# Halves of the split weight blocks over the contraction instead of the columns, in a kernel of two model blocks on one core

## What is computed

```python
for l in range(2):
    mod = silu(c) @ w_ada[l] + b_ada[l]
    shift, scale, gate = split(mod)
    h = rms_norm(x, g_pre[l]) * (1 + scale) + shift
    (cq, ckv, kr, za, qb, kb, vb, zb, qc, kc, vc, zc, gcols) = split_cols(h @ w_in[l], IN_SPLITS)
    o_a = (mla_branch(cq, ckv, kr, ...) * silu(za)) @ w_o_mla[l]
    o_b = (swa_branch(qb, kb, vb, ...) * silu(zb)) @ w_o_swa[l]
    o_c = (diff_branch(qc, kc, vc, ...) * silu(zc)) @ w_o_diff[l]
    g = sigmoid(gcols).reshape(B, S, 3, D)
    y = (g[:, :, 0] * o_a + g[:, :, 1] * o_b + g[:, :, 2] * o_c) @ w_out[l]
    x = x + gate * rms_norm(y, g_post[l])
```

## Time and profile before

| | us |
|---|---|
| median of 3 runs | 1274.35 |
| lowest and highest run | 1274.13, 1277.66 |
| the profiled execution | 1275.58 |
| its span, first to last instruction | 1273.7 |
| busy in the span: PE | 1176.4 |
| PEld | 907.3 |
| DVE | 666.0 |
| ACT | 430.2 |
| POOL | 285.7 |

### The profile page before, as it was taken

The page is one execution under the profiler, slowest core; times in us unless marked ns, Lnnn a source line. Parts: engine busy times, 40 slices in busy tenths (PEclk is TensorE's granted clock), DMA queues, the critical chain, the costliest instruction groups (busy, mean ns, idle before and its releaser), DMA issues.

```text
span 1273.7 us, 18043 instructions
## 1 busy us (share of the span) xinstructions
PE 1176.4 (92%) x7403; PEld 907.3 (71%) x7403; DVE 666.0 (52%) x1091; ACT 430.2 (34%) x1041; POOL 285.7 (22%) x275
## 2 busy tenths in 40 slices
PE   7999999999897799789979999999898999999987
PEld 6888754677675422132268999998788799899877
DVE  3755866333883200010072556577785255667875
ACT  4759542334643200000055413304324431320432
POOL 0322331330510200000032122242452113224240
PEclk9999999999899899999989999999998999999999
DMA  7433435786129999999984444253321535334310
GB/s 214 175 133 125 160 99 165 270 292 237 68 83 416 410 422 421 421 421 421 413 193 140 155 158 166 99 199 133 132 98 65 188 110 195 141 116 157 125 67 33
DMA packets 94692, 255.97 MB, mean 201 GB/s; under 512 B 9873, under 2 KB 16322, under 8 KB 82322
## 3 DMA queue, kind: packets, MB, share of 16 engines
q1 hardware_dynamic: 90844, 251.18, 53.5%
q0 software_dynamic: 1152, 3.06, 0.8%
q10 hardware_dynamic: 2614, 0.59, 0.3%
HBM read 251.96 MB, written 2.59 MB: 200 GB/s over the span
## 4 chain that ended last, share of the span: by engine, by line
PE 61%; DVE 16%; DMA 12%; ACT 6%; SPq 2%; issue 2%; POOL 1%; ACTq 0%; DVEq 0%; POOLq 0%
PE bank L771 57%; DVE ring_r L2171 3%; PE bank L780 3%; DVE acc L2276 3%; SPq L691 2%; DMA place<-in_w_gate_dram 2%; DMA w_hi<-in_w_gate_dram 2%; DMA ring<-in_w_down_dram 2%; DMA ring<-in_w_up_dram 2%; DMA ring<-in_w_out_dram 1%; ACT L1644 1%; DMA ring<-in_w_ada_dram 1%; DVE ring L2286 1%; ACT ring L1644 1%; ACT oa L1644 1%
## 5 line engine op out<-in xcount | busy, mean ns | idle before, releaser
L2987 POOL CAST w_hi_r<-ring 128x1024 fp32r<-128x1024 f32 x136 | 151.9, 1145 | 629.0 <-DMA ring<-in_w_in_dram 258.3
L771 PE MATMUL bank<-ring_r,xT_hi 128*128 128x256 f32 (+1 forms) x864 | 242.6, 281 | 0.0
L2171 DVE TENSOR_TENSOR ring_r<-ring,w_hi_r 128x1024 fp32r<-128x1024 f32 x136 | 184.9, 1389 | 52.0 <-POOL w_hi_r L2987 52.0
L771 PE MATMUL bank<-w_hi_r,xT_hi 128*128 128x256 f32 x704 | 204.7, 291 | 6.8 <-DVE xT_r L2176 3.7
L771 PE MATMUL bank<-w_hi_r,xT_r 128*128 128x256 f32 x704 | 199.4, 283 | 0.0
L771 PEld LDWEIGHTS bank<-ring_r,xT_hi 128*128 128x128 f32 x864 | 164.7, 191 | 0.2
L771 PEld LDWEIGHTS bank<-w_hi_r,xT_hi 128*128 128x128 f32 x704 | 133.7, 190 | 19.0 <-issue 9.3
L771 PEld LDWEIGHTS bank<-w_hi_r,xT_r 128*128 128x128 f32 x704 | 133.2, 189 | 0.0
L771 PE MATMUL bank<-xT,ring 128*128 128x256 f32 x576 | 126.4, 380 | 0.0
L771 PEld LDWEIGHTS bank<-xT,ring 128*128 128x128 f32 x576 | 109.2, 191 | 15.3 <-issue 0.6
L2276 DVE SCALAR_TENSOR_TENSOR acc<-raw,cols,acc 128x256 f32<-128x256 f32 x168 | 87.9, 530 | 28.9 <-ACT acc L1644 23.8
(11 more groups left out here) (403 smaller groups left out, 2237.7 us busy)
## 6 DMA issues: line engine op xcount, KB each, us to landing
ring<-in_w_in_dram SPq DMA_DIRECT2D x38, 2048.0 KB, 7.8
ring<-in_w_ada_dram SPq DMA_DIRECT2D x12, 2048.0 KB, 8.8
ring<-in_w_up_dram SPq DMA_DIRECT2D x22, 1024.0 KB, 26.1
ring<-in_w_down_dram SPq DMA_DIRECT2D x20, 1024.0 KB, 25.3
ring<-in_w_gate_dram SPq DMA_DIRECT2D x18, 1024.0 KB, 20.9
ring<-in_w_out_dram SPq DMA_DIRECT2D x8, 2048.0 KB, 7.8
place<-in_w_gate_dram SPq DMA_DIRECT2D x6, 1024.0 KB, 26.8
bias<-in_w_up_dram SPq DMA_DIRECT2D x6, 1024.0 KB, 26.2
```

Source lines behind the costliest of these rows:

```text
L771: return release(nc.tensor.matmul(o, lhsT, rhs, start=start, stop=stop))
L2171: tt(lo, raw_, hi.bitcast(F32), ALU.subtract).then_inc(lo_done.sem, lo_done.one("piece"))
L2987: nc.gpsimd.tensor_copy(hi, raw_).then_inc(hi_done.sem, hi_done.one("piece"))
```

## The change

`by_rows(block)` is new. It holds for blocks of more than 2,048 elements a partition that are `w_out_2`, or `w_in_2` without the three blocks of `channel_job`. For them a part is no longer half of the columns over 8 k, but 4 k (`KH`) over all columns: part 0 is k 0 to 3, part 1 is k 4 to 7, each with one run of 2,048 elements in the ring. `row_sums` computes the 4 k of part `c` for a token tile into the whole width of the bank, starting the sum at k = 0 and ending it at k = 7, so a bank's sum now runs over both parts. `gate_sums`, `first_jobs`, the sections that aren't transposed, and `w_out_2` use it. A group is then 4 k by 3 matmuls, 12 in a row, of 512 columns (416 in the block at column 512). In `first_jobs` the wait for a tile's second half of k (x1 or x3) stands before k = 4, which is now the first matmul of part 1; in the very first part the wait for its second piece stands before k = 2. Pieces follow the parts: 2 k of 512 columns. Loads, homes, slots and the numbers of parts and pieces stay as they are.

```diff
--- before.py
+++ after.py
@@ -185,6 +185,13 @@
 
 
 SPLIT = ("w_in_2", "w_o_mla_2", "w_o_swa_2", "w_o_diff_2", "w_out_2")
+KH = DK // 2
+
+
+def by_rows(block):
+
+    name, _, _, k, c0, w = block
+    return k * w > HI and (name == "w_out_2" or name == "w_in_2" and c0 not in (SECTIONS[1][0][0], SECTIONS[2][0][0], SECTIONS[2][1][0]))
 
 
 SECTIONS = [[(0, 512), (512, 416)], [(928, 512), (1440, 256), (1696, 512)],
@@ -459,6 +466,9 @@
 
             n, i, m = parts_of[h]
             nk, w = plan[n][3], plan[n][5]
+            if by_rows(plan[n]):
+                return [v[slot[n]][:, i * KH * w:(i + 1) * KH * w].rearrange("p (k n) -> p k n", k=KH)
+                        for v in (ring, ring_r)] + [homes[hi_home[h][0]][:, 0:KH * w].rearrange("p (k n) -> p k n", k=KH)]
             return [v[slot[n]][:, 0:nk * w].rearrange("p (k n) -> p k n", k=nk)[:, :, i * w // m:(i + 1) * w // m]
                     for v in (ring, ring_r)] + [homes[hi_home[h][0]][:, 0:nk * w // m].rearrange("p (k n) -> p k n", k=nk)]
 
@@ -1345,11 +1355,16 @@
                                    k == 0, k == DK - 1)
                 last.then_inc(pj_pe.sem, pj_pe.one("job"))
 
+            def row_sums(w, t, c, o):
+
+                for k in range(KH * c, KH * c + KH):
+                    last = mm3(o, at(xs, every, k, slice(t * P, (t + 1) * P)), at(w, every, k - KH * c),
+                               k == 0, k == DK - 1)
+                return last
+
             def gate_sums(w, t, c, o):
 
-                for k in range(DK):
-                    last = mm3(o[:, c * T:(c + 1) * T], at(xs, every, k, slice(t * P, (t + 1) * P)), at(w, every, k),
-                               k == 0, k == DK - 1)
+                last = row_sums(w, t, c, o[:])
                 if c:
                     last.then_inc(gt_pe.sem, gt_pe.one("group"))
 
@@ -1388,12 +1403,12 @@
                     for c in range(m):
                         if t == 0:
                             ws.append(next_part(1 if part[0] == 0 else 2))
-                        for k in range(DK):
-                            if ws is sections[0] and c == 0 and k == DK // 2:
+                        for k in range(KH * c, KH * c + KH):
+                            if ws is sections[0] and k == KH:
                                 pe.wait_ge(xs_dve.sem, xs_dve.at(f"x{2 * t + 1}", l))
-                                if l == t == 0:
-                                    pe.wait_ge(lo_done.sem, 2)
-                            last = mm3(o[:, c * n // m:(c + 1) * n // m], at(xs, every, k, slice(t * P, (t + 1) * P)), at(ws[c], every, k),
+                            if ws is sections[0] and l == t == 0 and k == KH // 2:
+                                pe.wait_ge(lo_done.sem, 2)
+                            last = mm3(o[:, 0:n], at(xs, every, k, slice(t * P, (t + 1) * P)), at(ws[c], every, k - KH * c),
                                        k == 0, k == DK - 1)
                         if t:
                             part_read()
@@ -1436,11 +1451,8 @@
                             o = [job_bank(), job_bank(1)]
                             for c in range(m):
                                 w = next_part()
-                                n = section[0][2] // m
                                 for t in range(TT):
-                                    for k in range(DK):
-                                        last = mm3(o[t][:, c * n:(c + 1) * n], at(xs, every, k, slice(t * P, (t + 1) * P)),
-                                                   at(w, every, k), k == 0, k == DK - 1)
+                                    last = row_sums(w, t, c, o[t][:, 0:section[0][2]])
                                     if c == m - 1:
                                         last.then_inc(pj_pe.sem, pj_pe.one("job"))
                                 part_read()
@@ -1622,9 +1634,7 @@
                                 ws.append(next_part())
                             elif l < L2 - 1 and half and c:
                                 normed_transposes(l + 1, 0)
-                            for k in range(DK):
-                                last = mm3(bank[4 + 2 * half + t][:, c * T:(c + 1) * T], at(xs, every, k, slice(t * P, (t + 1) * P)),
-                                           at(ws[2 * half + c], every, k), k == 0, k == DK - 1)
+                            last = row_sums(ws[2 * half + c], t, c, bank[4 + 2 * half + t][:])
                             if t:
                                 part_read()
                         last.then_inc(w2_pe.sem, w2_pe.one("q"))
```

## The result

The changed kernel took 1267.47 us (median of 4 runs, 1266.24 to 1268.76), the kernel before 1275.05 beside it (4 runs, 1274.13 to 1277.66): ratio 0.9933, 95% interval 0.9914 to 0.9952 (the plain quotient of the two medians is 0.9941; ratios in this text are the record's). By the medians that is 7.6 us less. 1270.0 had been predicted, 4.4 us less. The gain is 1.7 times the forecast one by the medians and 1.9 times by the ratio, so terms of the sum were too small. Which ones is the subject of what follows. The profiled execution took 1266.58 us, its span 1264.8.

What follows compares the result with a forecast made beforehand. TensorE was taken to bound the attention units and last projection, DVE's weight split the stretch between the layers. Four terms summed to 4.4 us (1.3 to 5.4), from 1274.35 to 1270.0 us, range 1266.6 to 1273.8.

Steps and rivals of the forecast that it cites:

- The price of a pair: Two 256-column matmuls cost 0.2354 to 0.2370 us, one of 512 costs 0.2344: 0.0018 us saved a pair (0.0010 to 0.0026).
- Term 1: 38 groups in unbroken TensorE rows on the chain (first section, early gates, section blocks, w_out_2): 0.8 us saved (0.5 to 1.2).
- Term 2: 40 groups between the short matmuls of attention units, 0.04 us saved each: 1.6 us (0.8 to 2.0).
- Term 3: 416-column block for the second token tile, two groups a layer, 0.38 us saved each: 1.5 us (0 to 1.5).
- Term 4: 416-column block's second half, first token tile, layer 1, at the lower clock after idle: 0.5 us saved (0 to 0.7).
- What was put at nothing: Rest of the first tile's openings, other w_out_2 and gate groups, moved waits, DVE's and POOL's single runs, later releases: no effect.
- the signs that the prediction had named against itself: Wide steps above 0.237 us reading the ring, over 6 TensorE waits for the split, or the hole growing beyond TensorE's earlier saving.
- it only waits longer: Between the layers the chain runs over DVE's weight split, so a shorter TensorE group there saves nothing.
- Columns alone count: Rival: 416 columns cost twice 208, and a unit's group saves only 0.02 us; 1.6 us saved, 1272.7 us; chance 0.20.
- A clock episode vanishes: Rival: one low-clock episode after an idle, worth 1.4 us, disappears; 5.9 us saved, 1268.5 us; chance 0.10.
- A wide matmul steps like a narrow one: Rival: 512 columns step by 0.118 us, so 78 groups save 110 us, giving 1164 us; chance 0.01.
- The collision of DVE and POOL: Rival: single-run splits make both engines collide, 0.84 us more for each of 17 pieces on the chain; 1284.2 us; chance 0.06.

Runs made afterwards that it cites:

- e8: The changed kernel with unused rows of 48 matmuls of each width, 128 to 512 columns, added behind its last matmul: 1361.69 us (one run).
- e1: The changed kernel with its row halves kept, but wide products issued as two narrow ones again, except bank openers: 1275.18 us, ratio 1.0003 to the kernel before.
- e2: The kernel before with only the 416-column block cut by rows and multiplied wide: 1273.62 us, ratio 0.9983 to the kernel before.
- e4: The changed kernel unaltered, run again beside the kernel before: 1267.76 us, ratio 0.9939.
- e7: The changed kernel unaltered, run once more in the next batch, beside the filled kernels: 1266.82 us, ratio 0.9942 to the kernel before.
- e5: The changed kernel with unused matmuls filling TensorE's idle before two projections and in layer 1's opening: 1265.61 us, ratio 0.9928 to the kernel before.
- e6: The kernel before with the same idle places filled, by narrow matmuls in the opening: 1272.65 us, ratio 0.9983 to the kernel before.
- e11: The changed kernel with attention tiles moved by 32 bytes and the idle places filled: 1268.21 us, ratio 0.9933 to the kernel before.
- e12: As e11, with the expert stage's tiles moved to multiples of 64 bytes as well: 1268.69 us, ratio 0.9938 to the kernel before.

## Why the prediction was wrong in its size, and right in its direction

**The price of a pair** is the step that failed: 0.0018 us was taken (0.0010 to 0.0026), and the runs show 0.005 to 0.010. Both numbers of the difference were read from rows that don't stand for the others. "In rows 5 the 512-column form, which the branch output projection already has, goes 48 steps from 742.80 to 754.05: 0.2344" is true of that projection and was carried over to matmuls with another stationary tile, which step by 0.2300 (0.232 in the last projection). And the narrow step was taken from a unit and from the last projection, 0.1177 and 0.1185, where the long row from 757.00 steps by 0.1200. An error of 2% in one of two numbers of this size is several times their difference. "The time goes by columns, not by instructions" fell with it: e8 shows a fixed part, and e1 that the number of matmuls is the gain.

The terms can be measured in the profiled pair by how much earlier the same matmul starts.

**Term 1**, 0.8 us (0.5 to 1.2): mis-sized, and outside its bounds. The pieces that hold its 38 groups became 2.7 us shorter, without the 416-column block's share, 0.07 a group. The last projection gave 0.49 for 8 groups (23.03 to 22.54 us, where 22.7 to 22.8 had been forecast). The eight groups of the two section blocks gave 0.94 in layer 0 and 0.37 in layer 1: pieces of 37.07 and 39.84 us, then 36.73 and 39.61, all became 36.60 and 39.37. That is the narrow form's two steps: the rows within these pieces stepped by 0.1200 in layer 0 and by 0.1178 in layer 1. So part of this gain is that of one execution.

**Term 2**, 1.6 us (0.8 to 2.0): 1.7 was measured, by luck. Two errors cancel. In branches 0 and 1 a unit's piece became 0.06 shorter (its group 2.88 instead of 2.93 us), and 24 groups gave 1.5. In branch 2 sixteen groups gave 0.16 together, since TensorE does not set the pace there. DVE's last work on the probabilities of a unit there and the transposes that read them, before and after:

```profile
891.75 0.48 DVE L2733 SCALAR_TENSOR_TENSOR prob<-prob,ssum 128x256 f32<-128x256 f32 x1
...
892.29 0.44 PE L780 MATMUL bank<-eye,prob 128*128 128x128 f32 x2
```

```profile
887.72 0.48 DVE L2743 SCALAR_TENSOR_TENSOR prob<-prob,ssum 128x256 f32<-128x256 f32 x1
...
888.26 0.44 PE L790 MATMUL bank<-eye,prob 128*128 128x128 f32 x2
```

The transposes start 0.06 us behind DVE both times, and 0.21 us (before) and 0.38 us (after) behind the start of the last matmul of the gate group, where in branch 1 it is one step, 0.12 and 0.23. The unit takes 4.47 us before (887.82 to 892.29) and 4.48 after (883.78 to 888.26). The chain shows TensorE pieces all the same, because the last matmul's row still covers so short a wait: this is where the prediction's reading that a shorter group shortens the kernel in the units was wrong.

**Term 3**, 1.5 us: right. The step of 416 columns is 0.189 (0.1905 taken), a group 0.40 (0.38 taken), 1.6 us in all, and e2 agrees.

**Term 4**, 0.5 us: right in this pair, by luck in part. The block's second half took 4.31 us from 966.62 to 970.93, just as worked out, against 4.95; with a step of 0.346 at the lower level (0.345 taken). But the clock came back sooner elsewhere: 3.65 us for the same 12 in e4.

The four terms as measured are 2.7 + 1.7 + 1.6 + 0.6 = 6.6 us, beside the 6.5 of the pair. The median moved by 7.6, 7.5 (e4) and 7.4 (e7). The clock may account for some of the 0.9 that is left: one episode costs about 1.5 us and comes at one place or another in more than half of the cases. The narrow form's step may account for some too. Whether the changed kernel has fewer episodes by its own doing stays open: its executions had 0.983 to 0.985, 0.985 to 0.986 and 0.981 to 0.985 in three batches.

**What was put at nothing** stayed there, or nearly. DVE's and POOL's lines, as in the earlier trace rows, and TensorE's wait for the split, as in the earlier trace rows:

```profile
L2181 DVE TENSOR_TENSOR ring_r<-ring,w_hi_r x136: 1210/1218/2054, 642.8 to 1243.1; 128x1024 fp32r<-128x1024 f32 x136
...
L2997 POOL CAST w_hi_r<-ring x136: 1034/1043/2027, 636.0 to 1234.5; 128x1024 fp32r<-128x1024 f32 x136
```

```profile
PE bank L781 <- DVE ring_r L2181: 8.6, 7, 2.3
PE bank L790 <- DVE y L2648: 8.1, 2, 4.4
```

One run of 1,024 costs both engines what four of 256 did, to the nanosecond or two. TensorE waits 7 times instead of 6 and 0.7 us more in all: one of the signs that the prediction had named against itself came, at a small price. The hole between the layers is 4.36 us instead of 3.86, which is 0.5 of what TensorE had saved ahead of it: "it only waits longer" was the right reading, and the stretch that holds it gained 0.16 us.

**The rivals.** Columns alone count: no; 416 steps by 0.189, not by 0.222. A clock episode vanishes: yes, in the profiled pair, 1.46 us, and the price of 1.4 had been read rightly; as a steady difference between the kernels it isn't shown, and without it the pair gained 6.5 us by the change and not 4.4. A wide matmul steps like a narrow one: no. The collision of DVE and POOL: no, by the lines above and by e1.

## To carry to other kernels

Read the price of an instruction that a change will issue from rows with the same operands in the same tiles; a row of the same shape elsewhere may be 2% off, and where the gain is the difference of two forms, 2% is the gain. The first model's output projection, at 0.2313 in the trace before (45 steps from 360.63 to 371.04), would have been a second row here, and the narrow row from 757.00 a third; rows that disagree say how wide the term's bounds must be. A chain of TensorE pieces does not show that TensorE sets the pace: compare the start of the transposes with the end of what they read. Before adding up halves of a change under 1%, set executions to the same granted clock, or fill the idles behind which it falls; even at one clock two sets of runs of one kernel (e4, e7) lay 1.2 us apart here.

## What had not been expected of the hardware

- At the full clock a matmul of 256 columns or more costs a fixed part beside its columns: 0.120, 0.147, 0.174, 0.188, 0.200 and 0.230 us for 256, 320, 384, 416, 448 and 512 columns. 208 and 128 columns both cost 0.111 us.
- With the tokens' tiles a matmul of 512 columns steps by 0.2300 us, with the heads' tiles by 0.2343, whatever the tiles hold, and moving tiles by 32 bytes made 0.2332 and 0.2324 of it.
- A long row of 256 columns steps by 0.1178 or by 0.1200 us from one end to the other, and the same row of the same layer has either in different traces (7 of 12 rows at 0.1200).
- After 2.26 us of idle the low clock may come or not, in executions of the same kernel, and it may come three to five matmuls late; 1.88 us of matmuls put into the idle kept it away in all eight places traced (e5, e6, e11, e12).
